# Context tokens normalised and split during the expert value phase, and their key products put behind the gate

## The reference, cut to what matters

```python
h = h + peer_ffn(rmsnorm(h, ffn_norm), ...)              # 128 value matrices at its end
gate = sigmoid(rmsnorm(h, ple_gate_norm) @ ple_gate_w)
h = h + (p @ ple_proj) * gate                            # end of the first block
hc = ctx                                                 # 256 context tokens, an input
a_l = rms_norm(h,  norm_mix) * (1 + sc1_l) + sh1_l       # latent
a_c = rms_norm(hc, norm_mix) * (1 + sc1_c) + sh1_c       # context
qkv of a_l and of a_c with the same w_qkv (1024 x 3072)
```

## Time and profile before

| what | us |
|---|---|
| median of three runs | 2003.93 |
| profiled execution | 2005.8 |
| its span, first to last instruction | 2003.8 |
| PE busy | 1958.1 (98%) |
| DVE busy | 1446.1 (72%) |
| ACT busy | 1047.2 (52%) |
| mean granted TensorE clock | 0.991 |

### The profile page before, as it was taken

The page is one execution under the profiler, slowest core; times in us unless marked ns, Lnnn a source line. Parts: engine busy times, 40 slices in busy tenths (PEclk is TensorE's granted clock), DMA queues, the critical chain, the costliest instruction groups (busy, mean ns, idle before and its releaser), DMA issues. The chain is left out here.

```text
span 2003.8 us, 34025 instructions
## 1 busy us (share of the span) xinstructions
PE 1958.1 (98%) x13666; PEld 1726.6 (86%) x13666; DVE 1446.1 (72%) x2304; ACT 1047.2 (52%) x1979; POOL 34.5 (2%) x33
## 2 busy tenths in 40 slices
PE   8989999999999999999989999999999999999998
PEld 7869999999999888888787877888888888789998
DVE  7777599988997688888587768577764228776554
ACT  5675444478886555455573257442223117565544
POOL 0000000000000000000010000100000001000000
PEclk9989999999999999999999999999999999999999
DMA  7403566654455677777536420345673333125664
GB/s 252 155 17 116 185 187 188 189 177 151 157 159 174 204 265 257 256 252 249 170 123 215 158 80 17 102 144 196 243 276 107 105 95 106 39 93 165 185 190 126
DMA packets 94828, 326.92 MB, mean 163 GB/s; under 512 B 10320, under 2 KB 15824, under 8 KB 94672
## 3 DMA queue, kind: packets, MB, share of 16 engines
q1 hardware_dynamic: 94672, 324.75, 50.2%
HBM read 323.66 MB, written 1.05 MB: 162 GB/s over the span
## 5 line engine op out<-in xcount | busy, mean ns | idle before, releaser
L331 DVE TENSOR_TENSOR wlo<-raw,whi 128x1024 fp32r<-128x1024 f32 x502 | 612.6, 1223 | 312.4 <-ACT whi L325 309.3
L325 ACT ACTIVATE whi<-raw 128x1024 fp32r<-128x1024 f32 x502 | 526.0, 1050 | 375.2 <-PE ps L677 360.4
L675 PE MATMUL ps<-x_hi,whi 128*128 128x512 f32 (+1 forms) x976 | 332.5, 341 | 7.2 <-DVE x_lo L478 4.3
L676 PE MATMUL ps<-x_lo,whi 128*128 128x512 f32 (+1 forms) x976 | 329.2, 337 | 0.0
L677 PE MATMUL ps<-x_hi,wlo 128*128 128x512 f32 (+1 forms) x976 | 329.0, 337 | 0.0
L675 PE MATMUL ps<-xT_hi,whi 128*128 128x256 f32 x1136 | 323.2, 285 | 2.2 <-DVE xT_lo L476 1.9
L677 PE MATMUL ps<-xT_hi,wlo 128*128 128x256 f32 x1136 | 317.2, 279 | 0.0
L676 PE MATMUL ps<-xT_lo,whi 128*128 128x256 f32 x1136 | 317.0, 279 | 0.0
L675 PEld LDWEIGHTS ps<-xT_hi,whi 128*128 128x128 f32 x1136 | 213.6, 188 | 2.8 <-issue 1.7
L675 PEld LDWEIGHTS ps<-x_hi,whi 128*128 128x128 f32 x976 | 183.4, 188 | 35.4 <-issue 8.8
L676 PEld LDWEIGHTS ps<-xT_lo,whi 128*128 128x128 f32 x1136 | 213.8, 188 | 0.0
(11 more groups left out here) (447 smaller groups left out, 3277.3 us busy)
## 6 DMA issues: line engine op xcount, KB each, us to landing
raw<-peer_u_t SPq DMA_DIRECT2D x128, 512.0 KB, 3.6
raw<-peer_v_t SPq DMA_DIRECT2D x128, 512.0 KB, 4.1
raw<-ffn_in_t SPq DMA_DIRECT2D x88, 512.0 KB, 4.4
x<-ada_t SPq DMA_DIRECT2D x64, 512.0 KB, 4.5
raw<-ffn_out_t SPq DMA_DIRECT2D x44, 512.0 KB, 3.7
raw<-qkv_t SPq DMA_DIRECT2D x36, 512.0 KB, 4.4
gated<-ada_t SPq DMA_DIRECT2D x32, 512.0 KB, 6.0
raw<-w_in_t SPq DMA_DIRECT2D x24, 512.0 KB, 3.9
```

The source lines that it names most:

```text
L325: act.activation(whi[:, n % SPLIT, 0:w], raw[:, g % RAW, 0:w], ACT.Copy).then_inc(hi_done, 1)
L331: dve.tensor_tensor(wlo[:, n % SPLIT, 0:w], raw[:, g % RAW, 0:w], whi[:, n % SPLIT, 0:w].bitcast(F32), ALU.subtract).then_inc(lo_done, 1)
L675: pe.matmul(place, wh, xh, start=start, stop=False, skip_group_check=shared)
L676: pe.matmul(place, wh, xl, start=False, stop=False, skip_group_check=shared)
```

## The change: context work moved into the value phase

- **Space.** A tensor `kept` of 32 KB a partition replaces the first 32 gates; `h2`, `x2` and the context's split parts `ctx_parts` lie in it. `Gates` is a view over both tensors, so the routing operation of line 2200 is issued twice for each batch (gates 0 to 31, and the rest).
- **SP, value phase.** `ctx_t` is loaded twice (1 MB each): behind the load of piece 10, and behind that of piece 116, the second after all 32 halves are added. Between them SP waits for the context sums before it loads the first half.
- **Value phase work.** Squares at steps 16 to 19 (ACT), three Pool additions, sums at step 24 (PE), inverse root at step 27 (ACT, with the table load that stood at the end of the phase), scales at 118 to 121 (DVE), high parts at 121 to 124 (ACT), low parts at 122 to 125 (DVE). The first `ada` quad is written out at step 80 instead of 124, `finish_layer` for it follows at 82.
- **Gate stage.** Two SBUF to SBUF DMAs of 1 MB (`move_context`) replace the load of `ctx_t`. `out_at=1, halved=True`: sigmoids ahead of the split of the seventh piece, squares behind it, DVE two chunks on either side of it; PE's wait for tile 0 stands behind the column-wise products. The sigmoid table is preloaded.
- **Leading products.** `ContextLead` issues the context's 48 products from the finished parts (256 columns, banks 2 and 3), then the latent ones (48 of 258 columns). The norm is of 256 tokens only (`n == T`), with 4 Pool folds; the next 48 products keep 512 columns (`whole`).

```diff
             def _(sp):
                 loads(sp, at_v[8])
...
+                loads(sp, at_v[C + 2] + 1)
+                sp.wait_ge(gates_lo, C)
+                sp.dma_start(ctx_first, dr["ctx_t"]).then_inc(ctx_loaded, 16)
+                loads(sp, at_v[min(VALUE_HALVES) - 2] + 1)
+                sp.wait_ge(ctx_summed.h, ctx_summed.at(1))
                 for i in VALUE_HALVES:
                     loads(sp, at_v[i - 2] + 1)
                     load_half(sp, i)
+                loads(sp, at_v[max(VALUE_HALVES)] + 1)
+                sp.wait_ge(half_added.h, half_added.at(len(VALUE_HALVES)))
+                sp.wait_ge(quad_summed.h, quad_summed.at(1))
+                sp.dma_start(ctx_h, dr["ctx_t"]).then_inc(ctx_loaded, 16)
                 loads(sp, at_ple + RAW)
...
+                    if i == CTX_SUMS:
+                        pe.wait_ge(ctx_folded.h, ctx_folded.at(3))
+                        for n in range(2):
+                            mm = pe.matmul(ps[:, 7, 0:T], k("ones"), ctx_sq[:, n, :], start=(n == 0), stop=(n == 1))
+                        mm.then_inc(ctx_summed.h, 1)
...
+                    if i == CTX_INVERSE:
+                        ple_norm.load_table(act)
+                        act.wait_ge(ctx_summed.h, ctx_summed.at(1))
...
                 split_hi(act, at_proj)
-                ple_norm.load_table(act)
...
+                    for c in CTX_SCALED.get(i, ()):
+                        if c == 0:
+                            dve.wait_ge(ctx_loaded, 32)
+                            dve.wait_ge(ctx_rstd.h, ctx_rstd.at(1))
...
+                        for a, b in ((0, KEPT), (KEPT, i)):
+                            tokens_ = gbuf[:, a:b, BATCH * r:BATCH * r + BATCH]
...
-            def load_context(sp):
-                sp.dma_start(h2[:, :, T:TT], dr["ctx_t"]).then_inc(ctx_loaded, 16)
+            def move_context(sp):
+                for part, whole in zip(ctx_parts, x2H):
+                    sp.dma_start(whole[:, :, T:TT].bitcast(F32), part.bitcast(F32)).then_inc(ctx_loaded, 16)
...
+        class ContextLead(Lead):
+            def pe(self, pe, norm, folds):
+                pe.wait_ge(*self.moved)
+                for c in range(C):
+                    at = pieces[self.first + c // 4][3]
+                    if c % 4 == 0:
+                        pe.wait_ge(lo_done, at + 1)
+                    for j in range(2):
+                        w = c % 4 * 2 * P + j * P
+                        products(pe, self.context_place(j), [y[:, at % SPLIT, w:w + P] for y in (whi, wlo)], [y[:, c, :] for y in self.context],
+                                 c == 0, c == C - 1)
+                super().pe(pe, norm, folds)
```

More of the change, by code:

```diff
@@ L547, in __init__ @@
                 self.second = second
+                self.whole = None
                 self.more = 5
@@ L616, in pe @@
                         place, columns, share = self.second(j)
-                        mm = products(pe, place, [y[:, at % SPLIT, w:w + P] for y in (whi, wlo)], [y[:, c, columns] for y in norm.parts],
+                        mm = products(pe, place, [y[:, at % SPLIT, w:w + P] for y in (whi, wlo)], [y[:, c, columns] for y in self.whole or norm.parts],
                                       c == 0 and not (share and j), c == C - 1, share)
@@ L799, in _ @@
                             pe.wait_ge(dve_evacuated.h, dve_evacuated.at(d_out))
+                    if then:
+                        if woven:
+                            woven.pe(pe, len(ids))
+                        if not halved:
+                            last_freed()
                     if END:
@@ L844, in take_out @@
                                 job[3](act, filled(t, j)).then_inc(act_evacuated.h, 1)
-                        if then:
+                        if then and squared:
                             then.squares(act, spans[t - 1][1][-1][1] if t else 0, spans[t][1][-1][1])
@@ L881, in _ @@
                                     take_out(0)
-                                take_out(t - 1)
+                                take_out(t - 1, not halved)
+                            if halved and t >= 1 and i == out_at + 1:
+                                then.squares(act, 0, spans[t - 1][1][-1][1])
                             if woven:
@@ L899, in _, with take_out @@
                 def _(dve):
-                    def take_out(t):
+                    def take_out(t, some=slice(None)):
                         g0, outs = spans[t]
-                        for j, job in enumerate(tiles[t][3]):
+                        for j, job in list(enumerate(tiles[t][3]))[some]:
                             if lead and t == 0:
@@ L1958, in _ @@
             def _(pool):
+                pairs = ctx_sq.rearrange("p (c w) t -> p c (w t)", w=2)
+                for n in range(1, 4):
+                    pool.wait_ge(ctx_squared.h, ctx_squared.at(n + 1))
+                    if n >= 2:
+                        pool.wait_ge(ctx_folded.h, ctx_folded.at(n - 1))
+                    pool.tensor_tensor(pairs[:, 0, :], pairs[:, 0, :], pairs[:, n, :], ALU.add).then_inc(ctx_folded.h, 1)
                 ple_norm.pool(pool, VALUE_FOLDS, wide=2)
```

162 lines of the change are left out of this document (119 added, 43 removed).

## The result

The kernel after takes 2019.45 us (median of six runs, 2018.89 to 2022.51), the kernel before, beside it, 2004.14. The ratio is 1.0080, with an interval of 1.0069 to 1.0091. The forecast was 2006.6, the range ended at 2011: the time is outside it on the slow side. The profiled execution of after took 2019.71 with a span of 2017.5.

What follows compares the result with a forecast made beforehand. PE, busy in 98% of the span, was taken as the bound. Terms -6.3 - 0.5 + 0.3 + 1.0 + 0.2 + 0 + 6.4 + 1.6 = +2.7 on 2003.9 gave 2006.6 us; range 1997.5 to 2011, the forecast's own 2003.5 to 2009.

Steps and rivals of the forecast that it cites:

- The gap at step 117: Value phase: piece 117, issued behind the second context load, lands late and PE idles; +6.4 us (3.4 to 6.6).
- Rivals 1 and 2: 1: no gap at step 117, 1998.6 us, chance 0.20; 2: half a gap and the clock holds, 2002.0 us, chance 0.12.
- The clock behind it: Value phase after the gap at step 117: PE restarts at the lower clock; +1.6 us (0 to 3.3).
- rival 4: Gate gap of 2.8 us halves the clock; step 117's gap does for 6.8 us; +1.6 + 1.7, 2009.9 us, chance 0.17.
- Gate stage and key products: First gate product to last normalised one: 57.4 us becomes 51.1, with waits of 2.8 and 0.8 left; -6.3 us.
- rival 5: Gate stage: context products do not fill the gap, the eighth piece standing ahead; 2.8 us remain; no chance given.
- Moves: Two 1 MB SBUF copies ahead of the fifth gate piece in SP's queue delay it; +0.3 us (0 to 6).
- Rival 3: Slow SBUF copies make the fifth gate piece late, 6 us on top; 2012 us, chance 0.09.
- Context sums: Value phase, step 24: four records of 0.23 us on PE, with a restart; +1.0 us.
- The wait of piece 28: Value phase: SP's wait for the context sums delays the load of piece 28; +0.2 us (0 to 1).
- Table load: Moved from the value phase's end into ACT's idle time at step 27; -0.5 us.
- The routing operation in two: Value phase, DVE: 64 times an operation's fixed part, hidden in its waits for ACT; 0, at most 4.5 us.

Runs made afterwards that it cites:

- e1: The changed kernel without the 480-byte spacer ahead of gh and gl, so both are back at their old SBUF places; 2009.59 us, 1.0029 of before.
- e2: The kernel before with 480 bytes more of spacer ahead of gh and gl, nothing else; 2015.01 us, 1.0047 of before.
- e3: e1 with SP issuing pieces 117 to 120 before it waits for the last half and loads the context again; 2002.36 us, 0.9988 of before.
- e4: e3 with pieces 28 and 29 issued before SP waits for the context sums; 2003.03 us, 0.9988 of before.
- e7: Two runs of the kernel before with spacers putting gh and gl 32 or 64 bytes behind a multiple of 128; 2012.3 and 2014.7 us.
- e11: The kernel before with whi and wlo 64 bytes behind a multiple of 128, gh and gl on one; 2031.1 us.
- e12: The kernel before with whi, wlo, gh and gl all 64 bytes behind a multiple of 128; 2027.9 us.
- e14: The kernel before with whi and wlo 64 bytes and gh and gl 32 bytes behind a multiple of 128; 2028.5 us.
- e8: e4 with the gate stage's eighth weight piece split two turns earlier on ACT and DVE; 2003.21 us, 0.9994 of before.
- e5: e4 with the gate stage in the order of the kernel before and no sigmoid table preload; 0.9988 of before.

## Why the prediction was wrong, step by step

- **The step that failed.** The part on the value phase keeps the step of before: "PE takes 2.72 a step", with small terms beside it (-0.5, +1.0, +0.2, 0). It asks of each new instruction where it hides, and never what the new tensors move. The change's space part moves `gh` and `gl` from a multiple of 128 bytes to 96 behind one: **+9.8 us**, two thirds of the result. e1 and e2 show it from both sides. None of the five rivals had it either: it is no wait, and in the profile PE is just as busy. The spacers of odd widths ahead of `gh` and `h2` in the code of before were there to be asked about.
- **The gap at step 117** was forecast at 6.4 and is 6.3, by the named chain; e3 removes it. Rivals 1 and 2 fall.
- **The clock behind it**: the mechanism was right, the size was not: 2.8 instead of 1.6 (bounds 0 to 3.3). The low stretch was not that of the earlier trace rows: it reached from inside the gap to 977.5. This is nearer to the second half of rival 4 (6.8 us of low clock) than to the 1.6 that I took.
- **Gate stage and key products**: -6.1 against -6.3; the waits 2.86 and 1.09 against 2.8 and 0.8, no wait for tile 0, none for `x_lo`, no low clock. Rival 4's first half did not come. Of rival 5, the wait that it names remained.
- **Moves**: 0.3 forecast, none found; the copies took 4.9 and 8.1 us to landing, the piece behind them was in time, since PE waits for nothing between 1019.49 and 1040.08. Rival 3 falls.
- **Context sums** +1.0: steps 24 and 25 are 0.9 longer. **The wait of piece 28**: 0.2 forecast, 1.0 in the profile of after (steps 27 and 28), 0.9 to 1.0 in e3, nothing in e1, so it changes from run to run; e4 removes its cause. **Table load** -0.5: step 126 is 0.3 shorter, the end of the phase behind it as long as before.
- **The routing operation in two**: DVE's wait for ACT from 560 to 625 us is 1.9 where it was 2.3; nothing reaches PE there. The 0.3 that the attention behind it loses no experiment tied to it.
- **Two slips in its sums** changed nothing: 959.3 + 1.05 + 1.22 is 961.6, not 961.7, and rivals 3 and 4 with a fifth of the forecast make 0.34, not 0.32.

Summed, the terms I had make +20.4 - 9.8 - 6.1 = +4.5 us in place of +2.7; with the one I had not it is +14.3, and the measured difference is 15.3 (the spans of the two profiles differ by 13.7). e1, which lacks the missing term, took 2009.59: inside the range, and just above the 2009 of the forecast's own.

## What to carry to other kernels

When a change allocates, drops or resizes anything in SBUF, work out the start of every tile that a matmul reads, before and after, and treat each rest by 128 bytes that has changed as a term of the sum with a sign to be measured. For products of 512 columns a multiple of 128 was the best place in all rows compared here; for 256 columns it was not. Compare the median duration of an untouched group of products in both profiles first, for a wait-free slowdown of 3% shows in no list of waits. A transfer that must wait for something late in a phase belongs behind the loads the ring can still take, not ahead of them: that order alone was worth 9.0 us in the profile here and 7.2 by the runs. A reordering that moves a wait is worth something only if the sum of the waits or the clock gains by it: this one left the sum as it was, alone (6.1 and 6.2 us) and with the context's work gone (3.8 and 3.8), and gained 1.8 us in the profile only where it kept the clock up.

## What the runs showed of the hardware

- A value product of 128x512 in fp32r starts 0.227 us after the one before if its stationary and moving tiles both start on a multiple of 128 bytes, and 0.233 if either does not (e2, e7, e11). With weights as the stationary operand 64 off, products of 512 columns lose 2.2 ns (e11), and of 256 columns some lose 1.7 to 3.3 ns and some gain 2 to 5 (e11, e12, e14). The Trainium skill ("SBUF — State Buffer", "Operand start alignment") asks for a multiple of the element size and says that this is about legality, not speed; every place here is legal by it, and the runs show that speed depends on more.
- Copies of 1 MB within SBUF landed 4.9 and 8.1 us after issue when sent back to back; the load of 1 MB from HBM takes 5.8.
- An idle time of 6.1 us of PE left the clock at the lower level until 977.5, 6.1 us after PE had begun again; one of 4.0 us (e8) until about 1037.4, 5.4 us after. Waits of 2.86 us in after and 2.70 in e4 left it untouched, yet two of 1.61 and 1.67 with 0.9 us of work between them (e5) had a low stretch of 3.4 us behind them. In e3, with a wait of 2.92 at the place where after has 2.86, the clock fell 1.5 us after PE had begun again and stayed low to 1029.4, so the length of one gap does not tell alone:

```profile
1026.00:1029.30 3.30, 3.30 (x18) 3.30 (x17) 3.22 (x9) 1.30 (x4) 0.72 (x1) 0.50 0.76 286
```
